# Last keys' chain moved into the second projection, two column sums into other PSUM banks, six weight loads later in SyncE's queue

## The reference, cut to what matters

```python
# layer A: recurrent block
u = rmsnorm(x, norm_a) @ w_in_a                      # 1024 -> x branch | gate
xc = causal_conv(x_branch)                           # 4 taps
h = rglru(xc)                                        # two gate matmuls, scan over the frames
x1 = x + (h * silu(gate)) @ w_out_a
# keys and values, once, shared by layer B
k, v = split(rmsnorm(x1, norm_kv) @ w_kv)            # 128 | 128 columns, 2 heads of 64
k = rmsnorm_per_head(k) * k_norm
# layer B: attention in a window of 128 frames, with a sink per head
q, gate = split(rmsnorm(x1, norm_b) @ w_in_b)
q = rmsnorm_per_head(q) * q_norm
y = x1 + (attend(q, k, v) * silu(gate)) @ w_out_b
```

## Time and profile before

| | |
|---|---|
| median of 3 runs | 1495.9 us (1495.4 to 1502.24) |
| the profiled execution | 1499.04 us |
| its span, first to last instruction | 1497.3 us |
| mean granted TensorE clock | 0.994 of full speed |
| recurrent stage's last step to second projection | about 685 to 760 us of the span |

### The profile page before, as it was taken

One profiled execution on the slowest core, in us unless ns is written; L12 is line 12 of the kernel. 1 busy time (PEld: TensorE's weight loads), 2 busy tenths in 40 slices (PEclk: granted clock), 3 DMA queues, 4 the chain that ended last, 5 costly groups with the idle time before them and its releaser, 6 DMA issues.

```text
span 1497.3 us, 31229 instructions
## 1 busy us (share of the span) xinstructions
PE 1459.7 (97%) x10634; PEld 1400.7 (94%) x10634; DVE 1035.9 (69%) x2235; ACT 700.1 (47%) x1577; POOL 259.3 (17%) x203
## 2 busy tenths in 40 slices
PE   7999999999999999999899999999998999999999
PEld 7999999999999999998899999999986788888888
DVE  6987857665688888887884534435277877777771
ACT  5433423427787777773362423414145544444440
POOL 0011111001334434443170000000011111111110
PEclk9999999999999999999999999999999999999999
DMA  6565655659855545555523222122345444443312
GB/s 239 168 206 215 214 179 196 219 191 328 301 185 154 170 150 169 169 169 166 176 90 105 76 75 92 51 99 69 94 140 178 122 131 131 124 110 103 106 51 78
DMA packets 215218, 224.20 MB, mean 150 GB/s; under 512 B 61488, under 2 KB 201776, under 8 KB 215088
## 3 DMA queue, kind: packets, MB, share of 16 engines
q1 hardware_dynamic: 202960, 213.19, 45.6%
q10 hardware_dynamic: 12128, 9.39, 1.9%
HBM read 136.33 MB, written 86.44 MB: 149 GB/s over the span
## 4 chain that ended last, share of the span: by engine, by line
PE 63%; DVE 5%; ACT 2%; DMA 1%; issue 1%; SPq 0%; POOL 0%; DVEq 0%; ACTq 0%
PE s_banks L790 22%; PE bank L1812 11%; PE bank L1464 11%; PE s_banks L1431 5%; PE s_banks L1762 3%; PE bank L1447 3%; PE bank L1794 2%; PE bank L1777 2%; PE bank L790 2%; PE bank L1798 2%; ACT m_p L1988 1%; DVE m_nmax L1865 1%; PE bank L1780 1%; DMA x_dram<-r_x 1%; DMA r_x<-xT_dram 1%
## 5 line engine op out<-in xcount | busy, mean ns | idle before, releaser
L1988 ACT ACTIVATE m_p<-s_banks,m_nm 128x192 f32<-128x192 f32 (+2 forms) x264 | 106.1, 414 | 193.0 <-DVE m_nm L1869 193.0
L1812 PE MATMUL bank<-m_y_hi,w_hi_a 128*128 128x256 f32 (+1 forms) x512 | 148.9, 291 | 2.8 <-DVE w_lo_a L910 1.9
L1812 PE MATMUL bank<-m_y_lo,w_hi_a 128*128 128x256 f32 (+1 forms) x512 | 143.8, 281 | 0.0
L1812 PE MATMUL bank<-m_y_hi,w_lo_a 128*128 128x256 f32 (+1 forms) x512 | 143.7, 281 | 0.0
L790 PE MATMUL bank<-a_hi,w_hi_a 128*128 128x352 f32 x384 | 123.6, 322 | 1.3 <-DVE a_out L690 1.1
L790 PE MATMUL bank<-a_hi,w_lo_a 128*128 128x352 f32 x384 | 123.9, 323 | 0.0
L790 PE MATMUL bank<-a_lo,w_hi_a 128*128 128x352 f32 x384 | 123.9, 323 | 0.0
L790 PE MATMUL s_banks<-b_hi,w_hi_b 128*128 128x352 f32 x336 | 111.2, 331 | 0.0
L1464 PE MATMUL bank<-r_y_hi,w_hi_a 128*128 128x264 f32 x384 | 109.3, 285 | 0.6 <-ACT r_std L1359 0.6
L1464 PE MATMUL bank<-r_y_lo,w_hi_a 128*128 128x264 f32 x384 | 109.1, 284 | 0.0
L1464 PE MATMUL bank<-r_y_hi,w_lo_a 128*128 128x264 f32 x384 | 108.8, 283 | 0.0
(11 more groups left out here) (216 smaller groups left out, 4605.3 us busy)
## 6 DMA issues: line engine op xcount, KB each, us to landing
w_raw_b<-weights_dram SPq DMA_DIRECT2D x26, 512.0 KB, 4.3
w_raw_a<-weights_dram SPq DMA_DIRECT2D x25, 512.0 KB, 4.4
sga_dram<-a_out SPq DMA_DIRECT2D x48, 176.0 KB, 3.0
r_xc_hi<-xc_hi_dram SPq DMA_DIRECT2D x32, 264.0 KB, 3.0
r_xc_lo<-xc_lo_dram SPq DMA_DIRECT2D x32, 264.0 KB, 3.1
r_xc<-xc_dram SPq DMA_DIRECT2D x32, 264.0 KB, 3.8
r_sg<-sga_dram SPq DMA_DIRECT2D x32, 264.0 KB, 3.5
r_x<-xT_dram SPq DMA_DIRECT2D x64, 132.0 KB, 2.1
```

The lines of the kernel that those rows point to most:

```text
L1812: mm = nc.tensor.matmul(out_bank(ts, blk)[:, 0:width], w[pw][:, kt * P:(kt + 1) * P], (m.y_hi, m.y_lo)[px][tp][:, kt, 0:width], start=(n = ...
L1988: nc.scalar.activation(m.p[:, q, k, v0:192], s_banks[:, 2 * q + e, bp * 192 + v0:(bp + 1) * 192], ACT.Exp, bias=m.nm[:, q, k:k + 1], accum ...
```

## The change

- For tile 6 the token sum goes to bank 2 and the key sum to bank 3, which the gates used; both wait for the gates' last read in place of the waits on bank 5, and the output blocks 1 and 3 of tile 7 no longer wait for the roots. For tile 7 the key sum goes to bank 7.
- For tile 7 the square of k moves behind block 0 of the second projection on VectorE, the key sum behind block 2 on TensorE, the root behind block 2 on ScalarE, and the reciprocal and product behind block 3 on VectorE.
- The four unit loads at (8, 0) move down: two behind the x load of the first buffer, two behind that of the second.
- The two unit loads at the end of the stage move to blocks 4 and 5 of the projection's queue, and the store of k and v of tile 7 from block 4 to block 6.

```diff
--- before.py
+++ after.py
@@ -1010,7 +1010,15 @@
             t, pair, lag = (s - 1, g - 2, 1) if g >= 2 else (s - 2, g + 2, 2)
             return (t, 2 * pair) if known(s, lag, RN - 1 + lag) else None
 
+        def last_sums(t):
+
+            return isinstance(t, int) and t == RN - 2
+
         EARLY = {(PN, 2): 0, (PN, 6): 1, (PN, 8): 2, (PN, 11): 3, (PN, 13): 4}
+
+        def key_bank(t):
+
+            return 5 if not isinstance(t, int) or t < RN - 2 else 3 if t == RN - 2 else 7
 
         def early_turn(turn, n):
             s, g = divmod(n, NG)
@@ -1080,6 +1088,12 @@
                 t, blk = pair[0], pair[1] + q
                 eng.wait_ge(r.resid_done, NB * t + blk + 1)
                 eng.dma_start(x1_dst[:, blk, cols(t * RT, RT)], r.x1[:, q, :]).then_inc(r.x1_stored[q], 16)
+
+            def gates_free(s, g, first):
+
+                if isinstance(s, int) and (s, g) == (RN, 0):
+                    for k in (first, first + 1):
+                        load_unit(eng, U_B1 + k, r.gates_done, 4 * NG * RN)
 
             def load_next(pair, q):
                 t, blk = pair[0], pair[1] + q
@@ -1105,9 +1119,6 @@
                         load_gate(1, 0)
                     if isinstance(s, int) and (s, g) == (RN - 1, 0):
                         load_unit(eng, U_B1)
-                    if isinstance(s, int) and (s, g) == (RN, 0):
-                        for k in range(1, 1 + UNITS_GATE):
-                            load_unit(eng, U_B1 + k, r.gates_done, 4 * NG * RN)
                     if pair:
                         store_x1(pair, 0)
                         load_next(pair, 0)
@@ -1115,11 +1126,13 @@
                         load_gate(s, g)
                     if behind:
                         load_x(behind, 0)
+                    gates_free(s, g, 1)
                     if pair:
                         store_x1(pair, 1)
                         load_next(pair, 1)
                     if behind:
                         load_x(behind, 1)
+                    gates_free(s, g, 3)
                     if isinstance(s, int) and (s, g) == (RN, 2):
                         load_unit(eng, U_B1 + 7, r.out_done, NB * (RN - 1))
                     if known(s, 2, RN) and g == 3:
@@ -1164,11 +1177,20 @@
                                    (PN, 10): third, (PN, 12): fourth, (PN, 13): lambda: load_halves(1, 1),
                                    (PN, 15): lambda: load_halves(1, 2)})
             run_steps(eng, 2, RN - 2, RN + 2, body)
-            for u in range(U_OUT_B - 2, U_OUT_B):
-                load_unit(eng, u, r.kv_mm, NB * RN)
-
             for i in range(2):
                 eng.wait_ge(r.x1_stored[i], 16 * RN * NB // 2)
+
+        def key_square(eng, t):
+            eng.wait_ge(r.kv_read, 2 * t + 1)
+            need(eng, r.kms_done, t)
+            nc.vector.tensor_tensor(r.k2[:, :], r.k[:, :], r.k[:, :], ALU.mult).then_inc(r.k2_done, 1)
+
+        def key_norm(eng, t):
+            eng.wait_ge(r.kstd_done, t + 1)
+            nc.vector.reciprocal(r.std[:, :], r.std[:, :]).then_inc(r.krec_done, 1)
+            eng.wait_ge(r.krec_done, t + 1)
+            nc.vector.scalar_tensor_tensor(out=r.k[:, :], in0=r.k[:, :], scalar=vec[:, KN, 0:1], in1=r.std[:, :],
+                                           op0=ALU.mult, op1=ALU.mult).then_inc(r.k_done, 1)
 
         def recurrent_vector(eng):
             def one_minus(s, par, g):
@@ -1255,16 +1277,8 @@
                 nc.vector.tensor_tensor(r.k[:, :], bank[6][:, 0:RT], r.rstd[:, :], ALU.mult).then_inc(r.kv_read, 1)
                 need(eng, r.v_stored, 16 * t)
                 nc.vector.tensor_tensor(r.v[:, :], bank[7][:, 0:RT], r.rstd[:, :], ALU.mult).then_inc(r.kv_read, 1)
-                eng.wait_ge(r.kv_read, 2 * t + 1)
-                need(eng, r.kms_done, t)
-                nc.vector.tensor_tensor(r.k2[:, :], r.k[:, :], r.k[:, :], ALU.mult).then_inc(r.k2_done, 1)
-
-            def tail_norm(t):
-                eng.wait_ge(r.kstd_done, t + 1)
-                nc.vector.reciprocal(r.std[:, :], r.std[:, :]).then_inc(r.krec_done, 1)
-                eng.wait_ge(r.krec_done, t + 1)
-                nc.vector.scalar_tensor_tensor(out=r.k[:, :], in0=r.k[:, :], scalar=vec[:, KN, 0:1], in1=r.std[:, :],
-                                               op0=ALU.mult, op1=ALU.mult).then_inc(r.k_done, 1)
+                if not (isinstance(t, int) and t == RN - 1):
+                    key_square(eng, t)
 
             def turn(s, par, g):
                 one, two, pair = lagged(s, par, g, 1), lagged(s, par, g, 2), back_pair(s, g)
@@ -1280,8 +1294,8 @@
                     y_high(*two)
                 if known(s, 2, RN + 1) and g == 2:
                     tail_read(s - 2)
-                if known(s, 2, RN + 1) and g == 3:
-                    tail_norm(s - 2)
+                if known(s, 2, RN) and g == 3:
+                    key_norm(eng, s - 2)
                 if pair:
                     add_square(pair, 0)
                     residual(pair, 1)
@@ -1311,6 +1325,12 @@
             project_vector(eng, a1, after_project)
             run_recurrent(eng, turn, len(EARLY) + 1, RN + 2, after_slot)
             eng.wait_ge(r.x1_free, 1)
+
+        def key_root(eng, t):
+            eng.wait_ge(r.rstd_done, t + 1)
+            eng.wait_ge(r.kms_done, t + 1)
+            nc.scalar.activation(r.std[:, :], bank[key_bank(t)][:, 0:RT], ACT.Sqrt, scale=1.0 / HEAD,
+                                 bias=eps[:, 0:1]).then_inc(r.kstd_done, 1)
 
         def recurrent_scalar(eng):
             def multiplier(s, par, g):
@@ -1351,13 +1371,10 @@
                 if known(s, 2, RN + 1) and g == 2:
                     eng.wait_ge(r.ms_done, t + 1)
                     need(eng, r.k_done, t)
-                    nc.scalar.activation(r.std[:, :], bank[5][:, 0:RT], ACT.Sqrt, scale=1.0 / D,
+                    nc.scalar.activation(r.std[:, :], bank[2 if last_sums(t) else 5][:, 0:RT], ACT.Sqrt, scale=1.0 / D,
                                          bias=eps[:, 0:1]).then_inc(r.std_done, 1)
-                if known(s, 2, RN + 1) and g == 3:
-                    eng.wait_ge(r.rstd_done, t + 1)
-                    eng.wait_ge(r.kms_done, t + 1)
-                    nc.scalar.activation(r.std[:, :], bank[5][:, 0:RT], ACT.Sqrt, scale=1.0 / HEAD,
-                                         bias=eps[:, 0:1]).then_inc(r.kstd_done, 1)
+                if known(s, 2, RN) and g == 3:
+                    key_root(eng, t)
                 if known(s, 0, RN - 1):
                     gates(s, g)
                 for unit in recurrent_units(s, g):
@@ -1412,9 +1429,13 @@
 
         def key_sum(eng, t, last):
             eng.wait_ge(r.k2_done, t + 1)
-            if not last:
+            if last:
+                eng.wait_ge(r.kv_read, 2 * RN)
+            elif last_sums(t):
+                eng.wait_ge(r.gates_read, 4 * NG * RN)
+            else:
                 eng.wait_ge(r.resid_done, NB * (t + 1) + 2)
-            nc.tensor.matmul(bank[5][:, 0:RT], head_ones[:, :], r.k2[:, :], start=True, stop=True)\
+            nc.tensor.matmul(bank[key_bank(t)][:, 0:RT], head_ones[:, :], r.k2[:, :], start=True, stop=True)\
               .then_inc(r.kms_done, 1)
 
         def recurrent_tensor(eng):
@@ -1453,9 +1474,9 @@
                 mth = NB * t + blk
                 if blk == 0:
                     eng.wait_ge(r.y_low, NG * (t + 1))
-                if blk == 1:
+                if blk == 1 and not last_sums(t - 1):
                     need(eng, r.std_done, t)
-                if blk == 3:
+                if blk == 3 and not last_sums(t - 1):
                     need(eng, r.kstd_done, t)
                 split(eng, U_OUT_A + blk)
                 need(eng, r.resid_done, mth - 1)
@@ -1468,7 +1489,9 @@
             def token_sum(t):
                 eng.wait_ge(r.sq_added, NB * (t + 1))
                 eng.wait_ge(r.resid_done, NB * (t + 1))
-                nc.tensor.matmul(bank[5][:, 0:RT], ones[:, :], r.acc[:, :], start=True, stop=True)\
+                if last_sums(t):
+                    eng.wait_ge(r.gates_read, 4 * NG * RN)
+                nc.tensor.matmul(bank[2 if last_sums(t) else 5][:, 0:RT], ones[:, :], r.acc[:, :], start=True, stop=True)\
                   .then_inc(r.ms_done, 1)
 
             def turn(s, par, g):
@@ -1709,7 +1732,9 @@
                 eng.dma_start(m.xres[:, blk % 2, 0:AT], x1_dst[:, blk, cols((ts - 1) * AT + SAMPLE, AT)])\
                    .then_inc(m.xres_loaded[blk % 2], 16)
 
-            project_sync(eng, b1, {(1, 4): lambda: store_memory(eng, RN - 1), (1, 12): store_states, (PN, 0): start,
+            project_sync(eng, b1, {(1, 4): lambda: load_unit(eng, U_OUT_B - 2, r.kv_mm, NB * RN),
+                                   (1, 5): lambda: load_unit(eng, U_OUT_B - 1, r.kv_mm, NB * RN),
+                                   (1, 6): lambda: store_memory(eng, RN - 1), (1, 12): store_states, (PN, 0): start,
```

(8 more changed lines are left out.)

## The result

The change makes the kernel slower: 1507.68 us, median of 6 runs (1505.59 to 1510.24), against 1497.5 (1495.4 to 1502.24, 6 runs) for the kernel before. The ratio is 1.007, with a 95% interval of 1.0056 to 1.0084. The spans of the profiled executions are 1505.7 and 1497.3. The forecast was 1489.5, with a range from 1485.5 to 1494, so the kernel came out 18.2 us above the forecast and 13.7 above the range.

A forecast was written before the change was run, and what follows sets the result against it. TensorE, busy 97% of the span, was taken as the bound, so edits gain only the idle time they end there. 1.5 + 2.4 + 1.7 − 0.2 + 1.1 − 0.1 = 6.4 us off the median 1495.9: 1489.5 us, range 1485.5 to 1494.

The forecast's parts named there:

- The 3.13: TensorE's wait for a residual block before the projection, 3.13 us, which the forecast said no edit touches.
- −0.1 us (0 to −0.4, by a slower low part): GpSimd's head-matrix rewrite waits for the later key sum, with block 4's low part behind it: −0.1 us.
- the first part of the sum: Moving four weight loads behind the x loads starts TensorE's first block of tile 7 earlier: 1.5 us (1.3 to 2.4).
- TensorE has four banks: In the projection, four banks at 3.8 us per block cover VectorE's 2.3 us of added work at block 3.
- VectorE gets the square at block 0, the reciprocal and the product at block 3 … so nothing waits for VectorE: In the last keys' chain, VectorE's moved work in the projection costs nothing; the chain's gain was put at 1.1 us.
- TensorE does not wait: At tile 7's block 0, VectorE starts 1.2 us late but ends at 704.1, before TensorE needs its result at 705.4.
- some 5.4 us forecast at block 0 of the projection: Block 0 of the second projection was to start 5.4 us earlier: 1.5 + 2.4 + 1.7 − 0.2.
- the term of −0.2 (0 to −1.1): VectorE's lag from later x loads in tile 7, mostly paid by its idle time: −0.2 us, −1.1 the whole lag.
- The term of 2.4 for the clock: TensorE's lower clock in tile 7's first block is avoided by shorter pauses: 2.4 us (0 to 2.4).
- The slower one (0.04): Rival, chance 0.04: in tile 7, two weight loads hold a store as long as four did; 1.8 us slower, 1497.7.
- The rival that named GpSimd and VectorE: Rival, chance 0.03: GpSimd, slowed by VectorE, makes block 4's low part a whole one late (2.4 us); 1491.9.
- both clock falls gone: Lower clocks behind 698 and 739 both avoided; with 2.4 for the first part, the range's low end, 1485.5.

The follow-up runs named there:

- run 7: The changed kernel with the last keys' chain at its old place and GpSimd's head-matrix rewrite held until projection block 2 is done; 1507.59 us, ratio 1.0066.
- run 1: The changed kernel with GpSimd's head-matrix rewrite behind the low part of unit 7 of the second projection instead of unit 3; 1503.44 us, ratio 1.0032.
- run 5: The changed kernel with GpSimd's rewrite behind unit 7 and the last keys' reciprocal and product behind block 2 instead of 3; 1501.25 us, ratio 1.0029.
- run 8: Run 5's kernel with the third and fourth of the four unit loads moved behind the x load of tile 7, block 0; 1501.56 us, ratio 1.0029.
- run 9: Run 2's kernel with two of the four unit loads moved one turn later, behind the first x load of (8, 1); 1499.62 us, ratio 1.0006.
- run 3: The kernel before with one added wait: GpSimd's head-matrix rewrite held until block 2 of the second projection is done; 1511.93 us, ratio 1.0088.
- run 10: Run 2's kernel with the four unit loads back in front of the store at (8, 0); 1496.72 us, ratio 0.9994.
- run 12: The kernel before with the x load put ahead of the unit load behind each store of tile 7; 1500.43 us, ratio 1.0023.
- run 2: The changed kernel with the last keys' square, sum, root and product back at their old places; 1499.0 us, ratio 1.0007.

## Why the prediction was wrong

**Right.** The store no longer stands behind four loads, and output block 0 of tile 7 starts 1.7 earlier (1.5 taken). The clock stayed up behind 698 in the profiled execution; with the first root gone, block 1 is 5.1 ahead, where 1.5 + 2.4 + 0.57 = 4.5 were taken. The 3.13 stayed, the last keys' wait went, and TensorE waited for no low part at block 4.

**Wrong, the step that decided: "−0.1 us (0 to −0.4, by a slower low part)"** for GpSimd's rewrite. It asked only whether TensorE would get block 4's low part in time, and TensorE did. It did not ask what GpSimd's late run of low parts would meet on VectorE. The rows were there: a scaling copy of 0.36 took 0.96 beside GpSimd, and that price was used in the first part of the sum. Here it added 1.3 to 2.2 us to each of five operations in blocks 3 and 4. VectorE was covered by "TensorE has four banks", but the query sum behind block 8 needs all of VectorE's work on the eight blocks. Measured: 8.32 of wait, and the lower clock behind it. Run 7 shows that this alone makes the loss; runs 1 and 5 show that moving the rewrite away returns a little more than half of it, since the low parts then meet other work of VectorE.

**Wrong: "VectorE gets the square at block 0, the reciprocal and the product at block 3 … so nothing waits for VectorE".** The chain left a place where TensorE did not wait for it. VectorE may start on the projection's first block only once SyncE has seen the last x1 store land, and after the change it stands idle there (VectorE's timeline after):

```profile
745.66 2.35 DVE L671 RECIPROCAL b_std<-b_std 128x352 f32<-128x352 f32 x1 [3.96 <-SPq L1110]
```

In the kernel before, the keys' square filled that time (744.08 to 746.50); the reciprocal and product followed (747.88 to 750.87), and TensorE waited for nothing of 0.25 us or more in the eight blocks after. That this is why run 5 is still 0.29% slower is argued, not shown.

**Wrong: "TensorE does not wait"** at tile 7's block 0. The working looked for the reader of x's own result, and that came in time by 0.2 us. It had the tail of tile 6 run later, but missed that the tail frees the banks of the K/V step. That cost 2.38 and a lower clock: of some 5.4 us forecast at block 0 of the projection 0.7 were left, so the term of −0.2 (0 to −1.1) was too small by more than 4. Runs 8 and 9 take the wait away, and then other waits on later residuals use the time up.

**The term of 2.4 for the clock** was read from one execution, 3.1 above the median, and taken over to the median whole. Of four profiled executions with the old loads two show a fall there (0.54 before, 0.74 in run 3) and two do not (runs 10 and 12); how many of the runs behind the medians have it is not known. The four moved loads, put at 1.5 + 2.4, show no gain: 1.0007 with them moved (run 2), 0.9994 with them in place (run 10), in intervals that overlap.

**The rivals.** The slower one (0.04) got its sign by luck: it had a pair of loads hold a store as long as four did, 7.45, and needed more than 6.8. The pairs held theirs for 5.4 and 5.1 (from the store's issue to the x load behind it), near the 4.8 that the forecast itself used, and that was not the larger loss. The rival that named GpSimd and VectorE had it the wrong way round: it let VectorE slow GpSimd.

**Two sums** of the working are loose, and neither decided anything: 0.08 + 2 × 0.4 + 2.44 is 3.3 and not 3.4, and both clock falls gone with 2.4 for the first part make 1486.9, which was widened to 1485.5.

**Open.** Why run 5 keeps 2.65 of the wait was followed to VectorE's collisions from block 0 on, but none was taken away by itself. A second buffer for the head matrix, which would free the rewrite from the key sum altogether, was not tried.

## What to carry to other kernels

When a step moves, list every engine that waits for it in program order, and then ask what the work queued there will run beside at its new time, not only whether its reader still gets it in time. Before the change VectorE had room for one slow operation per block; with two or three it had none. A gain ahead of a stretch that another engine sets is not kept: here some 5 us were ahead of tile 7's block 1 and 0.7 at the projection. A clock fall seen in one profiled execution is not yet a term of the sum: of four executions with the same loads ahead, two had it.

## What the runs showed of the hardware

- VectorE's operations of 0.5 us with two SBUF inputs do not run beside GpSimd's low parts of 2.4 us: they end 0.2 to 0.4 us after the low part has, so they take between 1.5 us (L644 before) and 2.7, by how much of it is left. VectorE's copy with one SBUF input is hit as well (2.54 in place of 0.33), its reciprocal is not (1.79 against 1.80).
- Once VectorE was late, the three engines settled into another order: GpSimd made two low parts one after the other (5.30 for both in after and run 7, with 3.25 us idle before them and 3.2 behind), and VectorE did not catch up before the query sum.
- Behind the wait of 8.32 TensorE was granted 0.50 for 3 us and 0.63 for the next 4, so that a wait of 8.3 cost 2.7 us more (−6.6 to −9.3 in the table).
- The length of a pause alone did not tell whether the clock fell behind it. Ahead of tile 7's first K/V step, 2.38 us in after was followed by 0.66 (707 to 712), and 2.01 us in run 7 by 1.00 (707.36 to 712).
